# Sliding attention and the preparation of the RWKV scan: from two stages to one, with their operations interleaved

## The reference

```python
def dilated_window_mix(q_raw, k_raw, v_raw):        # 1024 tokens, 4 heads of 64
    for window, dil in ((128, 1), (512, 4), (2048, 16)):
        o, lse = banded_causal_attention(stride_gather(q, dil), stride_gather(k, dil),
                                         stride_gather(v, dil), window // dil)
    wts = jax.nn.softmax(jnp.stack(lses, 0), axis=0)
    o = jnp.sum(wts[..., None] * jnp.stack(outs, 0), axis=0)

def rwkv7_mix(c, mu, w0, w2, a0, a2, g2, k_k, k_a, r_k, ...):
    cm = cf + (c_prev - cf) * mu                     # 1024 columns
    r, k, v, wd, ad, gd = jnp.split(cm, splits, axis=-1)
    w = -jax.nn.softplus(-(w0 + jnp.tanh(wd) @ w2)) - 0.5
    decay = jnp.exp(-jnp.exp(w))
    a = jax.nn.sigmoid(a0 + ad @ a2)
    g = jax.nn.sigmoid(gd) @ g2
    kk = heads(k * k_k)
    kk = kk / jnp.maximum(jnp.linalg.norm(kk, axis=-1, keepdims=True), 1e-12)
    k = k * (1.0 + (a - 1.0) * k_a)
    # then the scan over time, with bonus = sum(r * k * r_k) * v added to its output
```

## Time and profile before

| what | value |
|---|---|
| median of 3 runs | 3496.6 us (3492.58 to 3500.79) |
| the profiled execution: its own time | 3495.54 us |
| the profiled execution: its span | 3493.7 us |
| mean granted clock of TensorE in it | 0.942 |
| TensorE matmul busy | 3102.5 us (89%) |
| VectorE busy | 1692.3 us (48%) |
| ScalarE busy | 988.2 us (28%) |
| GpSimd busy | 288.4 us (8%) |

### The profile page before, as it was taken

How to read it: one execution, slowest core, us unless ns; L and a number is a source line. 1 busy time by engine, 2 the same in 40 slices (tenths; PEclk the granted TensorE clock), 3 DMA queues, 4 the chain that set the end, 5 groups by cost and what they waited for, 6 DMA issues and landing times. The chain is left out here.

```text
span 3493.7 us, 48539 instructions
## 1 busy us (share of the span) xinstructions
PE 3102.5 (89%) x17690; PEld 2227.6 (64%) x17691; DVE 1692.3 (48%) x2694; ACT 988.2 (28%) x1633; POOL 288.4 (8%) x420
## 2 busy tenths in 40 slices
PE   7998977779699999968999697668889999999988
PEld 5887766755333333336887696457667887888866
DVE  6221744452542132335111673565548765877554
ACT  5211222342344554432001433321322100211023
POOL 2000012410122222210000000000000000000000
PEclk9998988899799999989999899779999999999999
DMA  6331665934599598952331211100213332333232
GB/s 211 95 113 65 185 216 176 294 99 168 223 401 409 226 408 324 408 184 72 97 114 58 69 35 46 64 2 23 89 49 96 96 96 84 90 96 96 90 95 86
DMA packets 389561, 510.65 MB, mean 146 GB/s; under 512 B 45597, under 2 KB 295140, under 8 KB 386224
## 3 DMA queue, kind: packets, MB, share of 16 engines
q1 hardware_dynamic: 354816, 442.32, 37.5%
q10 hardware_dynamic: 23520, 42.21, 3.5%
q0 software_dynamic: 11088, 24.22, 1.9%
HBM read 448.45 MB, written 69.37 MB: 148 GB/s over the span
## 5 line engine op out<-in xcount | busy, mean ns | idle before, releaser
L2441 PE MATMUL exp_up_psum<-exp_w,exp_x 128*64 128x512 f32 x1536 | 347.6, 606 | 5.8 <-issue 5.1
L421 PE MATMUL in_ps_psum<-hN_hi,in_wh 128*128 128x512 f32 x720 | 284.5, 395 | 19.4 <-DVE in_wl L415 13.9
L421 PE MATMUL ffn_ps_psum<-hN_hi,up_wh 128*128 128x512 f32 x704 | 276.4, 393 | 9.8 <-DVE up_wl L415 4.9
L422 PE MATMUL in_ps_psum<-hN_lo,in_wh 128*128 128x512 f32 x720 | 282.1, 392 | 0.0
L423 PE MATMUL in_ps_psum<-hN_hi,in_wl 128*128 128x512 f32 x720 | 282.0, 392 | 0.0
L423 PE MATMUL ffn_ps_psum<-hN_hi,up_wl 128*128 128x512 f32 x704 | 274.6, 390 | 0.0
L422 PE MATMUL ffn_ps_psum<-hN_lo,up_wh 128*128 128x512 f32 x704 | 274.5, 390 | 0.0
L2441 PEld LDWEIGHTS exp_up_psum<-exp_w,exp_x 128*64 128x64 f32 x1536 | 108.0, 139 | 211.8 <-issue 210.7
L2364 DVE COPY exp_w<-hN 128x1024 f32<-128x1024 f32 x128 | 89.6, 700 | 260.5 <-PE exp_up_psum L2441 239.5
L413 DVE CAST in_wh<-in_w 128x1024 fp32r<-128x1024 f32 x45 | 31.2, 693 | 371.1 <-PE in_ps_psum L423 370.2
L2498 ACT ACTIVATE exp_w<-exp_w_raw_down 128x1024 f32 x188 | 185.3, 1056 | 37.5 <-DMA exp_w_raw_down<-in_expert_w_out 37.4
(11 more groups left out here) (691 smaller groups left out, 6130.7 us busy)
## 6 DMA issues: line engine op xcount, KB each, us to landing
exp_w_raw_up<-in_expert_w_in SPq DMA_DIRECT2D x128, 512.0 KB, 15.8
exp_w_raw_down<-in_expert_w_out SPq DMA_DIRECT2D x128, 512.0 KB, 15.5
hN<-in_expert_w_in SPq DMA_DIRECT2D x128, 512.0 KB, 15.8
up_w<-in_ffn_up SPq DMA_DIRECT2D x88, 512.0 KB, 3.9
in_w<-in_w_in SPq DMA_DIRECT2D x44, 512.0 KB, 4.2
up_w<-in_ffn_down SPq DMA_DIRECT2D x44, 512.0 KB, 3.5
ada_lent<-in_ada_w SPq DMA_DIRECT2D x8, 1024.0 KB, 8.6
ada_w<-in_ada_w SPq DMA_DIRECT2D x8, 1024.0 KB, 7.6
```

What stands on the lines that cost most here:

```text
L421: pe.matmul(out, r(w[0]), r(x[0]), start=start, stop=False)
L422: pe.matmul(out, r(w[0]), r(x[1]), start=False, stop=False)
L2441: mm = pe.matmul(pu[lanes(j), :, :], xt[:, c % (KT // 2), lanes(c // (KT // 2))], f[:, :, j * FH:(j + 1) * FH], start=c == 0, stop=c == KT ...
```

## The change

`stage_rwkv_prep` is gone, and its operations are put in `stage_windows`, between those of the attention. The tiles of the scan (`K.rk`, `K.rkG`) are allocated ahead of the merged stage.
- The queries are no longer padded: `win_q` is 128 x 2 x 1024, filled by one load, and `scores` multiplies the 64 partitions of a head. The two memsets go, and the result's transposes are evicted into the queries' tile.
- The temporaries of the preparation lie in the planes of `K.rk` and in the input tiles, since both stages' tiles must fit in SBUF together. Three input tiles serve all 8 pieces, so later loads wait for the last reader of the earlier one.
- PSUM: the two output tiles now share a bank, and TensorE's output u waits for scaling u - 1 instead of u - 2. All products of the preparation go one at a time through one bank (`pp`), 512 columns each, and a product waits for the eviction of the one before it.
- The sigmoids are split off from the evictions of the low-rank products: `low_rank` evicts with a bias or a copy, and `sigmoids()` later does four 128 x 1024 sigmoids in place. The table of exponentials is now the one that also has the logarithm; the sigmoids' table is loaded twice in between, and that of the exponentials after each.
- Every operation of VectorE's preparation is a `step`, that is, VectorE waits for its end. The clamp of the norm and the bonus are in two halves of 512 columns.

The places in the loop over u: VectorE, behind scaling u - 2, in u = 1 and 2 the mixes of the two low-rank inputs; 5 values(0); 6 keys(0); 8 receptance(0); 12 cumulated(0) and centred(0); 13 norms(0, 0) and adapted(0); 15 norms(0, 1); 16 bonus(0, 0); 17 alphas(0); 18 decayed(0), bonus(0, 1); 19 betas(0); 20 gated(0); 21 keys(1); 22 receptance(1), cumulated(1); 23 centred(1); 24 norms(1, 0), adapted(1); 25 values(1); 26 norms(1, 1); 27 bonus(1, 0); 28 alphas(1); 29 decayed(1); 30 betas(1), bonus(1, 1); 31 gated(1). ScalarE, behind the copy of u - 1: 3 low_rank_inputs; 5 to 10 two low_rank evictions each (one ahead of the copy); 9 squares(0); 11 sigmoids; 14 decays(0); 16 roots(0); 22 squares(1); 26 decays(1); 27 roots(1). TensorE: in u = 4 to 9 two low-rank products each, one behind the transposes and one behind the output; norm in 11, 13, 22, 24; bonus in 15, 17, 26, 28, all behind the output.

```diff
+
...
-        q, k = K.sb("win_q", [P, 4, T], stack=st), K.sb("win_k", [P, 2, T], stack=st)
+        q, k = K.sb("win_q", [P, 2, T], stack=st), K.sb("win_k", [P, 2, T], stack=st)
-        oT, oF = K.sb("win_oT", [P, NT, 256], stack=st), sb2("oF", [P, T])
+        oT, oF = K.sb("win_oT", [P, NT, 256], stack=st), [q[:, a, :] for a in U]
-        pt = K.ps("win_t", [P, 2, BANK], st)
-        po = [K.ps(f"win_out{u}", [P, BANK], st) for u in U]
+        pt, pout, pp = K.ps("win_t", [P, 2, BANK], st), K.ps("win_out", [P, 2, 64], st), K.ps("rp_product", [P, BANK], st)
+        po = [pout[:, u, :] for u in U]
+        raw = [sb(f"raw_{n}", [P, T + 1]) for n in ("r", "k", "v")]
+        d0, ep, emid = sb("diff", [P, T]), sb("e_pos", [P, T]), sb("e_mid", [P, NC + 1])
+        b, bm, en = (x[:, 1:T + 1] for x in raw)
+        plane = lambda n, i: K.rk[:, n, i, :]
+        ranks, gate, reset, rkr = plane(RK_ALPHA, 1), K.rk_y[:, 1, :], K.rk_y[:, 0, :], K.rk_y[:, 1, :]
...
-                sp.dma_start(k[:], qk[256:512, :].rearrange("(a p) t -> p a t", p=P)).then_inc(s_qk, 16)
-                for h in range(4):
-                    sp.wait_ge(s_zero, h % 2 + 1)
-                    r = slice(64 * (h % 2), 64 * (h % 2) + 64)
-                    sp.dma_start(q[r, h, :], qk[h * 64:(h + 1) * 64, :]).then_inc(s_qk, 16)
+                def raw_in(n, r):
+                    sp.dma_start(raw[n][:, 1:T + 1], cin[r:r + P, :]).then_inc(s_raw[n], 16)
+                for t, r in ((k, 256), (q, 0)):
+                    sp.dma_start(t[:], qk[r:r + 256, :].rearrange("(a p) t -> p a t", p=P)).then_inc(s_qk, 16)
                 sp.dma_start(wide[:], K.wide_dram[:, 0:T]).then_inc(s_mask, 16)
+                raw_in(0, RK_WD)
+                raw_in(1, RK_WD + P)
                 sp.dma_start(v[:], vT[:, 512:768].rearrange("(c t) v -> t c v", t=P)).then_inc(s_v, 16)
+                raw_in(2, 512)
+                sp.wait_ge(s_mix, 2)
+                raw_in(1, 256)
+                raw_in(0, 0)
+                sp.wait_ge(s_e, 2)
+                sp.wait_ge(s_em, 1)
+                sp.wait_ge(s_ep, 1)
+                raw_in(1, 256 + P)
+                raw_in(0, P)
+                sp.wait_ge(s_en, 1)
+                raw_in(2, 512 + P)
                 for a in U:
                     sp.wait_ge(s_fc[a], 1)
-                    sp.dma_start(out[a * P:(a + 1) * P, :], oF[a][:]).then_inc(s_st, 16)
+                    sp.dma_start(out[a * P:(a + 1) * P, :], oF[a]).then_inc(s_st, 16)
                 sp.wait_ge(s_st, 32)
...
+                        mm = pe.matmul(ps[u % 2][:, c, 0:w], q[row(h), a, n * P:(n + 1) * P], k[row(h), a, c * BANK:c * BANK + w], start=True, stop=True)
                     mm.then_inc(s_s, 1)
...
-                    if u >= 2:
-                        pe.wait_ge(s_n, u - 1)
+                    if u:
+                        pe.wait_ge(s_n, u)
                     for c in range(n + 1):
-                        mm = pe.matmul(po[u % 2][:, 0:64], pT[u % 2][:, c, :], v[:, c, h * 64:(h + 1) * 64], start=c == 0, stop=c == n)
+                        mm = pe.matmul(po[u % 2], pT[u % 2][:, c, :], v[:, c, h * 64:(h + 1) * 64], start=c == 0, stop=c == n)
+                def low_rank(m):
+                    i, h, j = LOW[m]
+                    if m == 0:
+                        pe.wait_ge(s_low, 2)
+                        pe.wait_ge(s_w, 48)
+                    else:
+                        pe.wait_ge(s_ppe, m)
+                    w, x = ((w2, ranks), (a2, ranks), (g2, gate))[j]
+                    pe.matmul(pp[:], w[:, i * P:(i + 1) * P], x[:, half[h]], start=True, stop=True).then_inc(s_pp, 1)
+
+                def norm(i, h):
+                    pe.wait_ge(s_sq, i + 1)
+                    pe.wait_ge(s_ppe, NORM(i, h))
+                    pe.matmul(pp[:], K.c("ones64"), ep[:, half[h]], start=True, stop=True).then_inc(s_pp, 1)
+
+                def bonus(i, h):
+                    pe.wait_ge(s_rkr, i + 1)
+                    pe.wait_ge(s_ppe, BONUS(i, h))
+                    pe.matmul(pp[:], K.c("ones64"), rkr[:, half[h]], start=True, stop=True).then_inc(s_pp, 1)
...
                     for c in range(n + 1):
                         mm = pe.transpose(pt[:, c // 4, (c % 4) * P:(c % 4 + 1) * P], sc[u % 2][:, c * P:(c + 1) * P], K.c("ident"))
                     mm.then_inc(s_pt, 1)
+                    if 4 <= u < 10:
+                        low_rank(2 * (u - 4))
                     if u + 2 < NU:
                         scores(u + 2)
                     if u:
                         output(u - 1)
+                    if 4 <= u < 10:
+                        low_rank(2 * (u - 4) + 1)
...
+                def mixed(n, times, dst, mu):
+                    x = raw[n]
+                    dve.wait_ge(s_raw[n], 16 * times)
+                    step(dve.tensor_tensor(d0[:], x[:, 0:T], x[:, 1:T + 1], ALU.subtract))
+                    step(dve.scalar_tensor_tensor(dst, d0[:], K.col("rwkv_mu_2", mu), x[:, 1:T + 1], ALU.mult, ALU.add))
+                    dve.sem_inc(s_mix, 1)
+                def cumulated(i):
+                    dve.wait_ge(s_z, 5)
+                    dve.wait_ge(s_sig, 4)
+                    step(dve.tensor_tensor_scan(b, reset, plane(RK_BG, i), 0.0, ALU.mult, ALU.add))
+
+                def centred(i):
+                    mid = chunks(b)[:, :, MID:MID + 1]
+                    step(dve.tensor_tensor(chunks(bm), chunks(b), mid.to_broadcast([P, NC, RK_CH]), ALU.subtract))
+                    step(dve.tensor_tensor(plane(RK_ALPHA, i), bm, plane(RK_BG, i), ALU.subtract))
+                    dve.sem_inc(s_ea, 1)
+
+                def norms(i, h):
+                    dve.wait_ge(s_pp, NORM(i, h) + 1)
+                    step(dve.tensor_scalar(plane(RK_BG, i)[:, half[h]], pp[:], 1e-24, None, ALU.max))
+                    dve.sem_inc(s_ppe, 1)
+                    dve.sem_inc(s_max, 1)
+
+                def adapted(i):
+                    step(dve.tensor_scalar(d0[:], plane(RK_KG, i), -1.0, K.col("rwkv_k_a_2", i), ALU.add, ALU.mult))
+                    step(dve.scalar_tensor_tensor(plane(RK_K, i), d0[:], 1.0, plane(RK_K, i), ALU.add, ALU.mult))
+                    step(dve.scalar_tensor_tensor(rkr, plane(RK_RHO, i), K.col("rwkv_r_k_2", i), plane(RK_K, i), ALU.mult, ALU.mult))
+                    dve.sem_inc(s_rkr, 1)
+
+                def alphas(i):
+                    dve.wait_ge(s_inv, 2 * i + 2)
+                    dve.wait_ge(s_e, 2 * i + 2)
+                    step(dve.tensor_tensor(plane(RK_B, i), plane(RK_B, i), plane(RK_BG, i), ALU.mult))
+                    step(dve.scalar_tensor_tensor(plane(RK_ALPHA, i), plane(RK_B, i), -1.0, plane(RK_ALPHA, i), ALU.mult, ALU.mult))
+
+                def decayed(i):
+                    dve.wait_ge(s_ep, i + 1)
+                    step(dve.tensor_tensor(plane(RK_RHO, i), plane(RK_RHO, i), ep[:], ALU.mult))
+                    step(dve.tensor_tensor(plane(RK_K, i), plane(RK_K, i), en, ALU.mult))
+
+                def betas(i):
+                    step(dve.tensor_tensor(plane(RK_B, i), plane(RK_B, i), plane(RK_KG, i), ALU.mult))
+                    step(dve.tensor_tensor(plane(RK_B, i), plane(RK_B, i), en, ALU.mult))
+                    dve.sem_inc(s_en, 1)
+                    dve.wait_ge(s_em, i + 1)
+                    step(dve.tensor_tensor(K.rkG[:, i, :], chunks(ep[:])[:, :, RK_CH - 1], emid[:, 1:NC + 1], ALU.mult))
+
+                def gated(i):
+                    g = K.rkG[:, i, :].unsqueeze(2).to_broadcast([P, NC, RK_CH])
+                    step(dve.tensor_tensor(chunks(plane(RK_KG, i)), chunks(plane(RK_K, i)), g, ALU.mult))
+                    step(dve.tensor_tensor(chunks(plane(RK_BG, i)), chunks(plane(RK_B, i)), g, ALU.mult))
+
+                def bonus(i, h):
+                    dve.wait_ge(s_pp, BONUS(i, h) + 1)
+                    step(dve.tensor_tensor(K.rk_bonus[:, i, half[h]], pp[:], plane(RK_V, i)[:, half[h]], ALU.mult))
+                    dve.sem_inc(s_ppe, 1)
+                for x in raw:
+                    dve.memset(x[:, 0:1], 0.0).then_inc(s_zc, 1)
+                dve.wait_ge(s_zc, 3)
...
...
+                def low_rank_inputs():
+                    act.wait_ge(s_mix, 2)
+                    act.preload_act_table_set("sigmoid_and_others")
+                    act.activation(ranks[0:64, :], ranks[0:64, :], ACT.Tanh).then_inc(s_low, 1)
+                    act.activation(gate, gate, ACT.Sigmoid).then_inc(s_low, 1)
+                    act.preload_act_table_set("natural_log_exp_and_others")
+
+                def low_rank(m):
+                    i, h, j = LOW[m]
+                    act.wait_ge(s_pp, m + 1)
+                    dst = (plane(RK_BG, i), plane(RK_KG, i), K.rk_gate[:, i, :])[j][:, half[h]]
+                    if j < 2:
+                        act.activation(dst, pp[:], ACT.Identity, bias=K.col(("rwkv_w0_2", "rwkv_a0_2")[j], i)).then_inc(s_ppe, 1)
+                    else:
```

(93 more changed lines are left out.)

239 lines of the change are left out of this document (76 added, 163 removed).

## The result

The changed kernel takes 3511.4 us (median, 3504.8 to 3518.1) against 3497.0 (3490.4 to 3507.0): ratio 1.0042 [1.0028, 1.0057], 15 us slower where I forecast 9 faster, and outside my range. The profiled execution took 3509.7 us with a span of 3507.9, before 3495.5 with 3493.7. All of those 14.2 us but 0.6 lie in the stretch that the change touches: from the first instruction of the merged stage to the scan's first matmul it takes 201.3 us, where the two stages took 187.7 and I forecast 179.4.

What follows compares the result with a forecast made beforehand. Two interleaved chains through TensorE, VectorE and ScalarE were taken to set the pace. Start 7.1, loop 165.2 (99.6 + 57.6 + 3 + 2 + 3) and end 7.1 gave 179.4 us against 187.7: 3488 us, range 3468 to 3505.

Steps and rivals of the forecast that it cites:

- The scores: TensorE's score matmuls on 64 partitions: costed the same as on 128; at most 23 us of TensorE or 11 on chains gained.
- The clock: Merged loop: longer share of TensorE at half speed costs 3 us; granted clock 0.8 to 0.9.
- The clock turns it slower: Rival, chance 0.2: TensorE at half speed, 1.4 us a unit; 3503 half so, 3525 throughout; sign: loop clock under 0.7.
- The share of half: Loop: 115.1 us of work put between two interleaved chains' links; half is paid, 57.6 us.
- The start: From the merged stage's first instruction to the first scores: 7.1 us, against 10.1 before.
- the zeroing: Stage start: dropping the queries' zeroing saves 3 us (bounds 0 to 4).
- The values' wait: Output 0 waits for the values' load, queued on SP behind mask and two input pieces: 2 us (0 to 4).
- The end: From the last scaling over transposes, evictions and stores to the next stage's first instruction: stays 7.1 us.
- Added work: Loop: preparation adds 66.4 us to VectorE, 17.2 to TensorE, 31.5 to ScalarE; VectorE then busy about 97, ScalarE 77.
- removed stage: Second stage goes: its barrier, its loads (first VectorE result after 3.6 us) and its 69 us.
- lumps: Uneven work, as in units 3 and 11, that both chains wait for costs all of itself: 3 us more (0 to 8).
- the longest hold: Sign in the loop: the longest hold lies between exponentials 11 and 13.

Runs made afterwards that it cites:

- e2: Changed kernel with the queries padded with zeros again, so scores use 128 partitions; 3498.8 us, ratio 1.0008 to the kernel before.
- e3: Changed kernel with TensorE's output products of unit u - 1 issued ahead of the scores of unit u + 2; 3499.7 us, ratio 1.0017.
- e5: e2 (merged, padded) with the output products issued ahead of the scores; 3485.3 us, ratio 0.9965.
- e1: Kernel before, still two stages, with only the queries unpadded and loaded in one transfer, no zeroing; 3565.0 us, ratio 1.0203.
- e9: Kernel before with each unit's scores computed twice, first on 64 partitions, then on all 128; 3532.3 us, ratio 1.0112.
- e8: Kernel before, two stages and padded, with only the output products issued ahead of the scores; 3490.2 us, ratio 0.9983.
- e11: Merged, padded, output-first kernel with scores doubled in 24 units, plus eight VectorE additions (10 us) in units 18, 20, 29, 31; 3495.9 us, ratio 0.9997.
- e4: e3 with every scores product but the first two units' computed twice on 64 partitions; 3514.9 us, ratio 1.0056.
- e10: Kernel before with each unit's scores computed twice, both times on 128 partitions; 3523.3 us, ratio 1.0077.

## Why the prediction was wrong

- **The scores (the step that failed).** "Unpadded queries have the same columns, so I cost the scores the same", with bounds of nothing and a gain of up to 11 us. The duration at full clock bears it out (1.98 against 1.88 us for four), but the term lacked its other side: with this form the clock, once lost, does not come back while TensorE is busy, and all of TensorE's work then runs at half speed. It costs 12.5 us of the merged loop (after against e2), 20.7 in the better order (e3 against e5), 67 in two stages (e1). This turns e2, no change, into a slower kernel. How much of the 12.5 is clock and how much the change of form itself, which e9 prices at 12.5 in a loop near full clock, is not parted: the merged loop is mostly at half clock, and TensorE is not always what it waits for.
- **The clock.** I allowed 3 us; the mean was to be 0.8 to 0.9 and was 0.68, under the mark of the rival "The clock turns it slower". Its time, 3503 with half of the units slow, is near the outcome, and its mechanism is half right: the clock falls behind TensorE's gaps. What fails is the argument that I held against it, "a busy TensorE got its clock back": with 64-partition scores it was busy 28.4 of 30 and 43.6 of 46 us and did not (e1: 60 of 60). The rival had not foreseen this either, since it put the slow units down to the bursts between VectorE's operations, and padded, with the same bursts, the kernel is at 0.80 as forecast. So that its time came near is luck; by its own 1.4 us a unit, 16 slow units beyond the forecast would be 3510.
- **The share of half.** With TensorE's form and order equal, 62.8 of 115.1 us are paid (e5 against e8), 55%; e2 against before gives 71.6, 62%; the changed kernel 84.1, 73%. These shares hold the change of clock too (0.96 to 0.85 from e8 to e5). So half was nearly right as an average where the scores are padded, and the 6.0 us by which e2's loop is over the forecast 165.2 are this and the clock together. It is an average: where a unit is full already, nearly all is paid (e11).
- **The start.** 9.0 us instead of 7.1. The 3 us for the zeroing were about right: e1, unpadded in two stages, starts at 7.5, 2.6 earlier than before, and the changed kernel 2.7 earlier than e2. The merged stage seems to start some 1.5 us later whatever the queries (9.0 against e1's 7.5, padded 11.7 against 10.1); with the spread of the starts that is barely shown, and its cause is open. The values' wait, forecast at 2 us, was 1.5.
- **The end.** 8.8 us to the scan's first matmul instead of 7.1. The two final sets of transposes took 1.97 and 1.91 us, 1.09 and 1.03 before: the clock again. In e3, where it is at full speed there, the end is 7.3.
- **Added work, removed stage, lumps.** VectorE 96.6 us (97 forecast) and ScalarE 75.0 (77) were right, and the second stage's barrier and loads are gone. The starts of units 11 and 12 are 7.8 us apart, but the longest hold is not there: in two half-speed units elsewhere (13 to 14, 22 to 23) it is 9.1 and 9.0. Units with VectorE's work start 3 to 9 us apart, where I had said 4.5 to 5.
- **The sum.** 179.4 + 1.9 (start) + 18.5 (loop: 12.5 form, 6.0 share and clock) + 1.6 (end) = 201.4, measured 201.3. It is a sum of measured differences, so that it closes proves nothing. (One slip in the chances: 0.17 and two thirds of 0.53 make 0.52, less a little, and not 0.54.) With the form left alone the outcome would have been no change, and not the forecast gain either: e2 is at 1.0008. I also missed what the order in TensorE's list is worth: 0.43% in the merged padded kernel (e2 to e5) and 0.17% in two stages (e8), where merging gives nothing in the old order (e2) and 0.18% in the new one (e8 to e5; these two intervals touch).

## What to carry to other kernels

Padding that only adds zeros to TensorE's unused rows is not waste: before taking it out, look at the granted clock of the loop. Where the clock falls, look for the gap ahead of it; where TensorE is busy and the clock still does not come back, ask in what form its matmuls come. Changing the form and merging stages are separate edits; measured together, a loss of some 12 us hid that the merge did no harm, and that with the output ahead of the scores it gains as much. Work put between the links of two interleaved chains costs a half to two thirds of itself on average here, and nearly all where the unit is already full.

## What the runs showed of the hardware

- Scores on 64 partitions leave TensorE at the lower of its two clocks though it has no idle time (e1: 60 of 60 us busy at 0.50, and no rise before the last two units), and the same scores with zeros in the other 64 partitions do not (before: 0.89, e8: 0.96). They need not take a full clock away (e4: 1.00 for 43 us with each score computed twice on 64 and twelve 128-partition products of the preparation between), and as many 128-partition scores beside them bring it up and hold it (e9: 0.95). What the chip measures is not shown by these runs.
- In both forms the clock fell behind idle time of TensorE: 1.2 to 4.1 of 7 us in 28 of 29 falls. Padded, it was back within 9 (e2), 10 (e5) and 13 us (before); with 64-partition scores it took up to 46 us (after), 40 (e3) and 36 (e4).
- A change between 64- and 128-partition matmuls costs about 0.4 us a unit near full clock (e9 against e10): 0.54 us pass ahead of the first load of the other form instead of 0.24. The Trainium skill, "TensorE: Matmul & The Clock Gate", section "Step-by-step: what each phase is for", has the load of the next weights pulled ahead of the running matmul. That e9's load comes 0.30 us later would fit one that is pulled ahead less, but no run here shows the cause.
